# 42 instead of 32 tokens by gathered rows, in three partition groups with three row slots

## The chip, the cores and the metric

The kernel runs on one core of one Trainium2 chip. The metric is the device time of one execution in microseconds (us). Three executions of the kernel before took 2955.79, 2960.62 and 2963.03 us; the median is 2960.62 us. A fourth one, taken by the hardware profiler, took 2955.81 us, and every row below comes from it.

## The reference, cut to what matters

Two transformer blocks are computed for 256 tokens of width 2048, in fp32. The change touches the last layer of the second block only, a mixture of 16384 experts. Each token chooses 16 experts in each of 8 heads, 128 in all, and gets from each a scalar activation and a row of 2048 values:

```python
    def block(args):
        xt, it, gt = args
        u = jnp.take(expert_u, it, axis=0)
        act = jax.nn.gelu(jnp.einsum('td,tkd->tk', xt, u)) * gt
        v = jnp.take(expert_v, it, axis=0)
        return jnp.einsum('tk,tkd->td', act, v)
```

`it` holds the 128 expert numbers of a token and `gt` their gate values. A final norm follows.

## The kernel before

**Two ways to the same layer.** Of the 256 tokens, the first `TD` = 224 go through the dense way: all 16384 experts are multiplied with them on TensorE, and a gate matrix that is zero wherever an expert was not chosen takes the unwanted ones out. The last `TS` = 32 tokens go through the sparse way: only their 128 chosen rows of u and of v are fetched, by gathers, and multiplied on VectorE (DVE).

**The dense way** streams u and v once, in 1 MB tiles (43, 43 and 42 of each, the three `RANGES`). The order is u0, v0, u1, v1, u2, v2, and I call each of these a pass. A tile is four pieces of 128 x 512, so the passes have 172, 172 and 168 pieces. Every fp32 weight is split in two parts, ACT makes the high part (`split_hi`, L266) and DVE the low part (`split_lo`, L274), for two pieces at a time. TensorE then does four pairs of matmuls in each piece. In a pair the high part meets both parts of the tokens, 2 x 224 = 448 columns, and the low part meets the high part of the tokens alone, 224 columns. In u passes that is `wide` (L292, L293), in v passes `experts_out` (L1406, L1408). ACT may split two pieces only when TensorE is done with the piece six before them (`NQ` = 8 pieces are held), and the DVE program puts the low part of piece s + 4 (`LA`) at the head of step s.

**Beside the pieces** each step s of a pass has other work at hand-set places. In u passes DVE adds the partial sums (`dve_u_sum`, L1349) and builds the gates of four tokens at a time (`dve_gates`, L1286 to L1297, `NG` = 56 per pass), and TensorE turns them into the gate matrix (`pe_gates`, L1311). In the first 36 pieces of a v pass DVE multiplies activation and gate (`dve_gated`, L1372, 12 pieces ahead of use) and takes the low part of the product (`dve_act`, L1388, 7 ahead). At 1, 44, 87 and 130 pieces it adds up v results (`dve_v_sum`).

**The sparse way.** 32 tokens stand four times over the 128 partitions, each group with 32 of the 128 experts of its tokens (`ROWS` = 32). One gather (`pool_rows`, L1447, issued by POOL) brings half a row, 4 KB, into each of the 128 partitions; 64 gathers bring u and 64 bring v. The gathered tile goes to one of two ring slots. `dve_rows` multiplies it: L1469 for u with a running sum, L1476 (L1473 the first time) for v. So one gather is one row operation, 128 in all. The next gather into a slot is issued when DVE is done with that slot. DVE does the row operation at its place in the list `PLACES` and not before: 16 and 15 places in u1 and u2, ten pieces apart; 36, 36 and 26 in the v passes, 3.5 pieces apart, of which the first stands 46 pieces into the pass. One of the places (`NROW`) is used to add the dot products, and gelu and gates follow on ACT and DVE. At the end TensorE adds the four groups (`pe_rows_sum`, L1551) and DVE adds the result to the last tokens.

**Queues.** All tiles of weights are issued by SP, in order, into three buffers `raw`; SP waits until the low parts of the tile three before are made. POOL's queue holds nothing but gathers in these passes.

Of the kernel before, what the change touches and what calls it, by code (L numbers as in the profile page):

```python
# [15 lines left out]
TS = 32  # L16
# [12 lines left out]
NR, NQ, LA = 3, 8, 4  # L29
# [84 lines left out]
def build(nc, A, out):  # L114
# [207 lines left out]
    norm_load = [("gp", 16), ("g2", 16), ("ffn_const", 32), ("g5", 16)]  # L322
# [806 lines left out]
    def dve_choice(e, s):  # L1129
# [53 lines left out]
        for n, tb in enumerate((1, 0)):  # L1183
# [14 lines left out]
            if d == 0:  # L1198
                e.wait_ge(S("tk"), TKN * 8)
                if n:  # L1200
                    e.wait_ge(S("sel"), 1)
                    e.wait_ge(S("sp_ix"), 2 + 3 * (128 // TS))
# [44 lines left out]
            elif d == 10 and n == 0:  # L1247
                own, ids = slice(TD - 128, 128), xi
                e.wait_ge(S("dec"), ND)
                e.scalar_tensor_tensor(ids[own, :], I_[own, :], 128.0, J_[own, :], ALU.mult, ALU.add).then_inc(  # L1250
                    S("sp_ix"), 1)
                e.wait_ge(S("sp_ix"), 1)
                e.tensor_scalar(ids[own, :], ids[own, :], 2.0, None, ALU.mult).then_inc(S("sp_ix"), 1)
                e.wait_ge(S("sp_ix"), 2)
                for j in range(128 // TS):
# [999 lines left out]
```

## Time and profile before

| | us |
|---|---|
| median of three runs | 2960.62 |
| profiled execution | 2955.81 |
| its span, first to last instruction | 2954.5 |
| of it, TensorE (PE) busy | 2911.7 |
| DVE busy | 2139.5 |
| ACT busy | 1570.7 |
| POOL busy | 419.0 |

Between the span and the time of the execution lie 1.3 us. A busy TensorE is one with a matmul in its pipeline, so this number says that it seldom stands still, not that it runs at its peak; the distance between the starts of two matmuls tells how fast it goes. The granted clock is 0.997 of full speed over the span. The page names a share of 9% of the chain that ended last for DMA, nearly all of it gathers.

### The profile page before, as it was taken

The page shows a single profiled execution, that of the slowest core. Times are in us where ns is not written, and L with a number is a line of the kernel's source. Part 1 is how long each engine was busy: PE and PEld are TensorE (multiplying, and loading weights), DVE is VectorE, ACT ScalarE, POOL GpSimd, SP SyncE. Part 2 cuts the span into 40 slices and gives each one's busy share as a digit, 9 for nine tenths or more (in the row PEclk, how much of TensorE's full clock was granted, in tenths as well). Part 3 has the DMA queues.
Part 4 walks back from the last instruction along what each step waited for, and adds up shares of the span by engine and source line. Part 5 has one row for each costly group of instructions (what it writes and reads, how often), then busy time and mean ns, then how long its engine had stood idle before and what let it go on. Part 6 is the DMA issues. An engine that isn't in the chain of part 4 may idle for free.

```text
span 2954.5 us, 45739 instructions
## 1 busy us (share of the span) xinstructions
PE 2911.7 (99%) x18502; PEld 2631.0 (89%) x18502; DVE 2139.5 (72%) x3352; ACT 1570.7 (53%) x2406; POOL 419.0 (14%) x304
## 2 busy tenths in 40 slices
PE   9999999999999999999998999999999999999998
PEld 7888888888888888899898999999999999999997
DVE  5566566666666455676589889778999777999776
ACT  4467755555555443577444556444556444556534
POOL 0011101111111000143020000232010133110131
PEclk9999999999999999999999999999999999999999
DMA  7544445555556554654564555788666788666784
GB/s 259 177 151 152 156 177 186 185 186 187 185 186 222 190 198 143 221 177 170 208 211 171 190 183 203 270 302 298 230 236 227 247 306 302 234 232 239 272 310 168
DMA packets 99009, 631.53 MB, mean 214 GB/s; under 512 B 11376, under 2 KB 12784, under 8 KB 31216
## 3 DMA queue, kind: packets, MB, share of 16 engines
q1 hardware_dynamic: 80368, 561.49, 54.3%
q0 software_dynamic: 18432, 67.12, 6.3%
q8 instruction: 148, 2.42, 0.3%
q14 instruction: 61, 0.50, 0.0%
HBM read 623.32 MB, written 4.19 MB: 212 GB/s over the span
## 4 chain that ended last, share of the span: by engine, by line
PE 78%; DMA 9%; DVE 8%; ACT 3%; issue 2%; SPq 0%; ACTq 0%; DVEq 0%
PE ps L292 26%; PE ps L293 13%; PE ps L1406 6%; PE ps L314 6%; PE ps L316 6%; PE ps L315 6%; DMA ring<-in_u_rows_dram,idx 5%; DMA ring<-in_v_rows_dram,idx 4%; PE ps L1408 3%; DVE loR L274 3%; PE ps L305 2%; PE ps L304 2%; PE ps L303 2%; ACT hiR L266 1%; PE ps L1311 1%
## 5 line engine op out<-in xcount | busy, mean ns | idle before, releaser
L274 DVE TENSOR_TENSOR loR<-raw,hiR 128x1024 fp32r<-128x1024 f32 x1017 | 1255.0, 1241 | 621.9 <-ACT hiR L266 618.4
L266 ACT CAST hiR<-raw 128x1024 fp32r<-128x1024 f32 x1026 | 1074.4, 1051 | 803.3 <-PE ps L1408 324.3
L292 PE MATMUL ps<-XA,hiR 128*128 128x448 f32 (+1 forms) x3936 | 1343.9, 391 | 10.7 <-DVE loR L274 9.3
L293 PE MATMUL ps<-XA,loR 128*128 128x224 f32 (+1 forms) x3936 | 1069.3, 272 | 0.0
L292 PEld LDWEIGHTS ps<-XA,hiR 128*128 128x128 f32 x3936 | 739.7, 188 | 127.1 <-DVE loR L274 6.6
L293 PEld LDWEIGHTS ps<-XA,loR 128*128 128x128 f32 x3936 | 747.7, 190 | 0.6
L1406 PE MATMUL ps<-hl,hiR 128*128 128x448 f32 x2048 | 651.0, 377 | 6.2 <-DVE loR L274 5.9
L1408 PE MATMUL ps<-hl,loR 128*128 128x224 f32 x2048 | 543.5, 265 | 0.0
L1406 PEld LDWEIGHTS ps<-hl,hiR 128*128 128x128 f32 x2048 | 385.2, 188 | 42.8 <-DVE loR L274 9.2
L1408 PEld LDWEIGHTS ps<-hl,loR 128*128 128x128 f32 x2048 | 392.1, 191 | 0.2 <-issue 0.2
L1447 POOL DMA_INDIRECT ring<-in_u_rows_dram,idx x64 | 103.2, 1612 | 716.8 <-DVE ring L1469 664.8
L1320 ACT ACTIVATE G__147<-ps 128x172 f32<-128x172 f32 (+1 forms) x168 | 52.9, 315 | 227.8 <-PE ps L1311 227.7
L1447 POOL DMA_INDIRECT ring<-in_v_rows_dram,idx x64 | 105.2, 1644 | 407.9 <-DVE vsum L1476 391.8
L314 PE MATMUL ps<-hiR,Y 128*128 128x512 f32 x344 | 133.8, 389 | 0.0
L315 PE MATMUL ps<-loR,Y 128*128 128x512 f32 x344 | 133.8, 389 | 0.0
L316 PE MATMUL ps<-hiR,Y 128*128 128x512 f32 x344 | 133.8, 389 | 0.0
L1469 DVE SCALAR_TENSOR_TENSOR ring<-ring,hrep 128x1024 f32<-128x1024 f32 x64 | 78.2, 1222 | 54.6 <-DMA ring<-in_u_rows_dram,idx 54.5
L1476 DVE SCALAR_TENSOR_TENSOR vsum<-ring,gated,vsum 128x1024 f32<-128x1024 f32 x62 | 79.5, 1282 | 47.5 <-DMA ring<-in_v_rows_dram,idx 47.4
L303 PE MATMUL ps<-XB,hiR 128*128 128x256 f32 x384 | 110.0, 286 | 0.0
L305 PE MATMUL ps<-XB,loR 128*128 128x256 f32 x384 | 108.6, 283 | 0.0
L304 PE MATMUL ps<-XB,hiR 128*128 128x256 f32 x384 | 108.6, 283 | 0.0
L314 PE MATMUL ps<-hiR,XA 128*128 128x512 f32 x256 | 101.0, 394 | 2.3 <-DVE loR L274 1.8
(307 smaller groups left out, 3490.1 us busy)
## 6 DMA issues: line engine op xcount, KB each, us to landing
raw<-in_u_dram SPq DMA_DIRECT2D x128, 1024.0 KB
raw<-in_v_dram SPq DMA_DIRECT2D x128, 1024.0 KB
raw<-in_w_up_dram SPq DMA_DIRECT2D x86, 1024.0 KB
raw<-in_w_down_dram SPq DMA_DIRECT2D x43, 1024.0 KB
raw<-in_w_in_qk_dram SPq DMA_DIRECT2D x32, 1024.0 KB
raw<-in_w_out_dram SPq DMA_DIRECT2D x32, 1024.0 KB
raw<-in_w_in_dram SPq DMA_DIRECT2D x24, 1024.0 KB
raw<-in_w_in_v_dram SPq DMA_DIRECT2D x16, 1024.0 KB
```

The lines of the kernel that those rows point to most:

```text
L266: e.copy(hiR[:, r:r + 2, :], raw[n % NR][:, q:q + 2, :]).then_inc(S("hi"), 1)
L274: e.tensor_tensor(loR[:, r:r + 2, :], raw[n % NR][:, q:q + 2, :], hiR[:, r:r + 2, :].bitcast(F32), ALU.subtract).then_inc(S("lo_pool" if p ...
L292: e.matmul(both, wh, X.hl[:, :, k, 0:nt], start=(k == 0), stop=False, skip_group_check=True)
L293: m = e.matmul(dst[:, 0:nt], wl, X.h[:, k, 0:nt], start=False, stop=(k == KC - 1), skip_group_check=True)
L303: e.matmul(dst, wh, X.h[:, k, :], start=(k == 0), stop=False)
L304: e.matmul(dst, wh, X.l[:, k, :], start=False, stop=False)
L314: e.matmul(dsts[tb], ah_, hi, start=first, stop=False)
L315: e.matmul(dsts[tb], ah_, lo, start=False, stop=False)
L316: m = e.matmul(dsts[tb], al_, hi, start=False, stop=last)
L1406: e.matmul(b[:, 0:2 * TD].rearrange("p (a t) -> p a t", a=2), wh, hl[:, :, i, :], start=(i == 0), stop=False, skip_group_check=True)
L1408: m = e.matmul(b[:, 0:TD], wl, hl[:, 0, i, :], start=False, stop=(i == i1 - i0 - 1), skip_group_check=True)
L1447: e.indirect_dma_start(ring[m % 2][:, :], None, A["u_rows" if m < NROW else "v_rows"], bass.IndirectOffsetOnAxis(ap=idx[:, m % NROW // 2, ...
```

## The change

`TS` becomes 42 and `TD` 214. Every pair of matmuls in the six passes has 428 + 214 columns instead of 448 + 224, and everything that is shaped by `TD` shrinks with it; the gates come in 54 groups per pass, the last with two tokens.

42 tokens fit three times into 128 partitions, so `GROUPS` is 3, a gather has 126 rows, and each group needs 43 of the 128 experts (3 x 43 = 129, the surplus one has gate 0). That makes 86 + 86 = 172 row operations, 44 more. The ring has three slots (`RN`). The places in u1 and u2 stay. Those in the v passes become 52, 51 and 39; they start 12, 3 and 3 pieces into the pass instead of 46, and stand 3.0, 3.2 and 3.4 pieces apart.

42 is no multiple of 32, so partitions 86 to 127 can't be copied to the groups by DVE. DVE writes indices and gates of all 128 tokens to a staging tile (six instructions instead of twelve), and SP copies them to the groups with six small DMAs. They stand in SP's queue behind the 13th tile of u0, with waits for `x_out` and `sp_ix`. The staging tile lies in the third ring slot. Sums at the end use all 128 partitions, with `sel4` zero where nothing is to be added, and two waits order them (`xacc`, `sp_x`). Two pairs of semaphores at the start of the kernel are merged (`gp` and `ident`; `x0sq` and `x1sq`). The rest of the diff is addresses and names.

```diff
-TS = 32
+TS = 42
...
-NR, NQ, LA = 3, 8, 4
+NR, NQ, LA, RN = 3, 8, 4, 3
...
-ROWS = 128 * TS // 128
+GROUPS = 128 // TS
+GP = GROUPS * TS
+ROWS = -(-128 // GROUPS)
 NROW = 2 * ROWS
 PLACES = [P_U[r] + 4 + 10 * k for r in (1, 2) for k in range((16, 15)[r - 1])]
-PLACES += [P_VV[r] + NI + 3 + int(3.5 * k) for r in range(3) for k in range((36, 36, 26)[r])]
+PLACES += [P_VV[r] + (12, 3, 3)[r] + int((3.0, 3.2, 3.4)[r] * k) for r in range(3) for k in range((52, 51, 39)[r])]
...
-    ring = [at(f"ring{i}", 4 * i, [128, 1024]) for i in range(2)]
-    SG = NI * TD / 256
+    
+    SG = -(-NI * TD // 8) / 32
     S_, G_ = at("S_", RB, [128, NI, TD]), at("G_", RB + SG, [128, NI, TD])
-    hl = at("hl", RB, [128, 2, NI, TD], F32R)
+    hl = at("hl", RB, [128, 2, int(SG * 256)], F32R)[:, :, 0:NI * TD].rearrange("p a (i t) -> p a i t", t=TD)
...
-    yT = [at("yT0", 8, [128, 8, TD]), at("yT1", o + 10.25, [128, 8, TD])]
-    idx = at("idx", 15, [128, ROWS, 2], U32)
-    gs = at("gs", 15.25, [128, ROWS])
-    dots = at("dots", 15.375, [128, ROWS, 2])
-    gated = at("gated", 15.625, [128, ROWS])
+    hrep, vsum = at("hrep", o + HV, [128, D]), at("vsum", o + HV, [128, D])
+    yT = [at("yT0", 8, [128, 8, TD]), at("yT1", o + HV + 8, [128, 8, TD])]
+    idx = at("idx", 14.75, [128, ROWS, 2], U32)
+    gs = at("gs", 15.125, [128, ROWS])
+    dots = at("dots", 15.3125, [128, ROWS, 2])
+    gated = at("gated", 15.6875, [128, ROWS])
+    ring = [at(f"ring{i}", (0, 4, o + HV + 14.75)[i], [128, 1024]) for i in range(RN)]
+    ixs = at("ixs", o + HV + 14.75, [128, GROUPS * ROWS, 2], U32)
+    gss = at("gss", o + HV + 16, [128, GROUPS * ROWS])
     o = RB + SG
     qT = [at(f"qT{i}", o - 16 + i, [128, T]) for i in range(16)]
     g5 = at("g5", o, [128, D])
...
-                own, ids = slice(TD - 128, 128), xi
+                ids = xi
                 e.wait_ge(S("dec"), ND)
-                e.scalar_tensor_tensor(ids[own, :], I_[own, :], 128.0, J_[own, :], ALU.mult, ALU.add).then_inc(
-                    S("sp_ix"), 1)
+                e.scalar_tensor_tensor(ids[:, :], I_[:, :], 128.0, J_[:, :], ALU.mult, ALU.add).then_inc(S("sp_ix"), 1)
                 e.wait_ge(S("sp_ix"), 1)
-                e.tensor_scalar(ids[own, :], ids[own, :], 2.0, None, ALU.mult).then_inc(S("sp_ix"), 1)
+                e.tensor_scalar(ids[:, :], ids[:, :], 2.0, None, ALU.mult).then_inc(S("sp_ix"), 1)
                 e.wait_ge(S("sp_ix"), 2)
-                for j in range(128 // TS):
-                    part, cs = slice(TS * j, TS * j + TS), slice(ROWS * j, ROWS * j + ROWS)
-                    e.tensor_copy(idx[part, :, 0], ids[own, cs]).then_inc(S("sp_ix"), 1)
-                    e.tensor_scalar(idx[part, :, 1], ids[own, cs], 1.0, None, ALU.add).then_inc(S("sp_ix"), 1)
-                    e.tensor_copy(gs[part, :], g_[own, cs]).then_inc(S("sp_ix"), 1)
+                e.tensor_copy(ixs[:, 0:128, 0], ids[:, :]).then_inc(S("sp_ix"), 1)
+                e.tensor_copy(ixs[:, 128:129, 0], ids[:, 127:128]).then_inc(S("sp_ix"), 1)
+                e.tensor_scalar(ixs[:, 0:128, 1], ids[:, :], 1.0, None, ALU.add).then_inc(S("sp_ix"), 1)
+                e.tensor_scalar(ixs[:, 128:129, 1], ids[:, 127:128], 1.0, None, ALU.add).then_inc(S("sp_ix"), 1)
+                e.tensor_copy(gss[:, 0:128], g_[:, :]).then_inc(S("sp_ix"), 1)
+                e.memset(gss[:, 128:129], 0.0).then_inc(S("sp_ix"), 1)
             elif d == 14:
                 e.wait_ge(S("sel_g"), 3 * n + 3)
                 e.scalar_tensor_tensor(selb[:, 3, half(tb)], bank[4][:, 256:384], 4096.0, selb[:, 2, half(tb)],
...
-    NG = TD // 4
+    NG = -(-TD // 4)
...
         if s == min(SLOT) - 14:
-            e.wait_ge(S("sp_ix"), 2 + 3 * (128 // TS))
-            e.wait_ge(S("x_out"), 16)
-            todo = [0, 1]
-        elif m is not None and m + 2 < 2 * NROW:
+            e.wait_ge(S("sp_load"), 32 * GROUPS)
+            todo = list(range(RN))
+        elif m is not None and m + RN < 2 * NROW:
             e.wait_ge(S("sp_use"), m + 1)
-            todo = [m + 2]
+            todo = [m + RN]
         for m in todo:
-            e.indirect_dma_start(ring[m % 2][:, :], None, A["u_rows" if m < NROW else "v_rows"],
-                                 bass.IndirectOffsetOnAxis(ap=idx[:, m % NROW // 2, m % 2:m % 2 + 1], axis=0)).then_inc(
-                S(f"row{m % 2}"), 16)
+            e.indirect_dma_start(ring[m % RN][0:GP, :], None, A["u_rows" if m < NROW else "v_rows"],
+                                 bass.IndirectOffsetOnAxis(ap=idx[0:GP, m % NROW // 2, m % 2:m % 2 + 1],
+                                                           axis=0)).then_inc(S(f"row{m % RN}"), 16)
 
...
-            e.wait_ge(S(f"row{m % 2}"), 16 * (m // 2 + 1))
-            rg, cs = ring[m % 2][:, :], slice(1024 * (m % 2), 1024 * (m % 2) + 1024)
+            e.wait_ge(S(f"row{m % RN}"), 16 * (m // RN + 1))
+            rg, cs = ring[m % RN][0:GP, :], slice(1024 * (m % 2), 1024 * (m % 2) + 1024)
...
-            m = e.matmul(bank[v_bank(2, 2) + f][:, :], sel4[:, :], vsum[:, quarter(f)], start=True, stop=True)
+            m = e.matmul(bank[v_bank(2, 2) + f][:, :], sel4[0:GP, :], vsum[0:GP, quarter(f)], start=True, stop=True)
...
+            if f >= 2 and tb:
+                e.wait_ge(S("sp_x"), 4)
...
-        load(e, "ident", ident[:, :], A["ident"])
+        load(e, "gp", ident[:, :], A["ident"])
...
-                for j in range(128 // TS):
+                for j in range(GROUPS):
                     load(e, "hrep", hrep[TS * j:TS * j + TS, :], tmp3[TD - 128:128, 1, :])
+            elif n == P_U[0] // 4 + 12:
+                e.wait_ge(S("x_out"), 16)
+                e.wait_ge(S("sp_ix"), SP_IX)
+                for j in range(GROUPS):
+                    own, to, cs = slice(TD - 128, 128), slice(TS * j, TS * j + TS), slice(ROWS * j, ROWS * j + ROWS)
+                    load(e, "sp_load", idx[to, :, :], ixs[own, cs, :])
+                    load(e, "sp_load", gs[to, :], gss[own, cs])
             elif n == P_VV[2] // 4 + 4:
```

What the change does to the queues, at three places. TensorE first, at the end of u0 and the start of v0; before:

```order
L293 MATMUL ps<-XA,loR 128x224
L292 MATMUL ps<-XA,hiR 128x448
L293 MATMUL ps<-XA,loR 128x224
L1406 MATMUL ps<-hl,hiR 128x448
L1408 MATMUL ps<-hl,loR 128x224
```

and now:

```order
L300 MATMUL ps<-XA,loR 128x214
L299 MATMUL ps<-XA,hiR 128x428
L300 MATMUL ps<-XA,loR 128x214
L1415 MATMUL ps<-hl,hiR 128x428
L1417 MATMUL ps<-hl,loR 128x214
```

The order is the same, and each matmul is narrower. (`XA` and `hl` are the tokens' side, `hiR` and `loR` the weights.)

DVE at the start of v1, from one low part to the next. `G_` is the product of activation (`S_`) and gate, `hl` its two parts. Before:

```order
L274 TENSOR_TENSOR loR<-raw_50,hiR 128x1024
L1349 TENSOR_TENSOR S__146<-S__146,ps 128x224
L1372 TENSOR_TENSOR G__147<-S__146,G__147 128x224
L1388 TENSOR_TENSOR hl<-G__147,hl 128x224
L1372 TENSOR_TENSOR G__147<-S__146,G__147 128x224
L1388 TENSOR_TENSOR hl<-G__147,hl 128x224
L274 TENSOR_TENSOR loR<-raw_51,hiR 128x1024
```

and now:

```order
L281 TENSOR_TENSOR loR<-raw_50,hiR 128x1024
L1358 TENSOR_TENSOR S__144<-S__144,ps 128x214
L1381 TENSOR_TENSOR G__145<-S__144,G__145 128x214
L1397 TENSOR_TENSOR hl<-G__145,hl 128x214
L1381 TENSOR_TENSOR G__145<-S__144,G__145 128x214
L1397 TENSOR_TENSOR hl<-G__145,hl 128x214
L1477 SCALAR_TENSOR_TENSOR ring_166,dots<-ring_166,hrep 126x1024
L281 TENSOR_TENSOR loR<-raw_51,hiR 128x1024
```

A row operation has come in between two low parts, in the stretch in which each piece also has its two operations on `G_` and `hl`.

POOL, from the last work of the layer before to the first gathers, with the semaphores that each waits for; before:

```order
L274 TENSOR_TENSOR loR<-raw_51,hiR 128x1024 [waits s_hi]
L1447 DMA ring_144<-in_u_rows_dram,idx 128x1024 [waits s_x_out,s_sp_ix]
L1447 DMA ring_145<-in_u_rows_dram,idx 128x1024
L1447 DMA ring_144<-in_u_rows_dram,idx 128x1024 [waits s_sp_use]
L1447 DMA ring_145<-in_u_rows_dram,idx 128x1024 [waits s_sp_use]
```

and now:

```order
L281 TENSOR_TENSOR loR<-raw_51,hiR 128x1024 [waits s_hi]
L1455 DMA ring_164<-in_u_rows_dram,idx 126x1024 [waits s_sp_load]
L1455 DMA ring_165<-in_u_rows_dram,idx 126x1024
L1455 DMA ring_166<-in_u_rows_dram,idx 126x1024
L1455 DMA ring_164<-in_u_rows_dram,idx 126x1024 [waits s_sp_use]
L1455 DMA ring_165<-in_u_rows_dram,idx 126x1024 [waits s_sp_use]
```

Three gathers go out before the first wait for DVE, and the first of them waits for SP's small DMAs.

## Rows read from the trace of the kernel before

**Rows 1.** The page: busy time of TensorE; the high-part group of ACT.

```profile
PE 2911.7 (99%) x18502; PEld 2631.0 (89%) x18502; DVE 2139.5 (72%) x3352; ACT 1570.7 (53%) x2406; POOL 419.0 (14%) x304
...
L266 ACT CAST hiR<-raw 128x1024 fp32r<-128x1024 f32 x1026 | 1074.4, 1051 | 803.3 <-PE ps L1408 324.3
```

**Rows 2.** Six passes: us, PE, PEld, DVE, ACT, POOL busy, PEclk, DMA share, GB/s.

```profile
1565.00:1816.00 251.00, 241.76 (x1836) 223.33 (x1837) 220.82 (x472) 134.73 (x252) 2.05 (x2) 0.99 0.54 185
1816.00:2037.00 221.00, 218.46 (x1379) 206.20 (x1378) 167.86 (x230) 100.24 (x121) 59.24 (x35) 1.00 0.79 285
2037.00:2271.00 234.00, 232.31 (x1824) 216.25 (x1823) 218.07 (x353) 128.71 (x236) 24.85 (x17) 1.00 0.68 234
2271.00:2495.00 224.00, 220.73 (x1382) 208.01 (x1381) 170.67 (x211) 99.95 (x122) 60.41 (x35) 0.99 0.78 282
2495.00:2722.00 227.00, 227.00 (x1793) 211.63 (x1793) 211.93 (x329) 125.97 (x232) 22.62 (x15) 1.00 0.68 232
2722.00:2941.00 219.00, 218.64 (x1377) 205.21 (x1376) 164.43 (x191) 100.54 (x131) 47.22 (x27) 1.00 0.72 259
```

**Rows 3.** Timeline of TensorE, wide pairs of an earlier layer: start, us, instruction; five starts.

```profile
699.61 0.40 PE L292 MATMUL ps<-XA,hiR 128*128 128x512 f32 x1
...
701.02 0.40 PE L292 MATMUL ps<-XA,hiR 128*128 128x512 f32 x1
```

**Rows 4.** The same view in v2; thirteen starts of L1406, first and last.

```profile
2740.09 0.38 PE L1406 MATMUL ps<-hl,hiR 128*128 128x448 f32 x1
...
2743.87 0.38 PE L1406 MATMUL ps<-hl,hiR 128*128 128x448 f32 x1
```

**Rows 5.** The same view in u1, around the matmuls of one gate group.

```profile
2180.38 0.37 PE L1311 MATMUL ps<-OG,OJ 128*128 128x43 f16 x8
2180.59 0.45 PE L292 MATMUL ps<-XA,hiR 128*128 128x448 f32 x1
```

**Rows 6.** Waits of TensorE over the six passes: us, times, longest.

```profile
PE ps L292 <- DVE loR L274: 9.0, 10, 1.8
PE ps L1406 <- DVE loR L274: 5.9, 7, 2.7
```

**Rows 7.** Timeline of DVE at the start of v0, two pieces.

```profile
1820.84 1.22 DVE L274 TENSOR_TENSOR loR<-raw,hiR 128x1024 fp32r<-128x1024 f32 x1
1821.97 0.39 DVE L1372 TENSOR_TENSOR G__147<-S__146,G__147 128x224 f32<-128x224 f32 x1
1822.28 0.39 DVE L1388 TENSOR_TENSOR hl<-G__147,hl 128x224 fp32r<-128x224 f32 x1
...
1823.18 1.22 DVE L274 TENSOR_TENSOR loR<-raw,hiR 128x1024 fp32r<-128x1024 f32 x1
```

**Rows 8.** Timeline of DVE in u2, around one row operation.

```profile
2502.30 1.28 DVE L1476 SCALAR_TENSOR_TENSOR vsum<-ring,gated,vsum 128x1024 f32<-128x1024 f32 x1
2503.50 1.22 DVE L274 TENSOR_TENSOR loR<-raw,hiR 128x1024 fp32r<-128x1024 f32 x1
```

**Rows 9.** The chain through v0: gathers from release to landing, shortest and longest of twelve.

```profile
1907.85 6.50 DMA ring<-in_u_rows_dram,idx
...
1944.09 10.08 DMA ring<-in_u_rows_dram,idx
```

**Rows 10.** Waits over v0 (1816 to 2036 us): waits of DVE for gathers.

```profile
DVE ring L1469 <- DMA ring<-in_u_rows_dram,idx: 38.4, 20, 5.8
```

**Rows 11.** DMA view, 1900 to 2030 us of v0: GB/s in 40 slices; packets, MB, share of engines.

```profile
GB/s 290 272 302 387 325 263 349 326 224 386 232 287 277 393 261 401 277 52 408 425 306 403 335 117 382 295 325 378 146 239 418 343 334 425 218 417 328 342 418 90
...
q1 hardware_dynamic: 3488, 25.34, 52.4%
q0 software_dynamic: 4086, 14.84, 31.7%
```

**Rows 12.** DMA view, first 40 us of the kernel: GB/s in slices of 1 us.

```profile
GB/s 0 57 172 426 459 401 410 426 467 366 461 426 401 418 483 393 410 333 228 262 418 355 392 377 412 389 410 434 442 98 8 0 0 0 16 172 418 410 401 393
```

More of the change, by code:

```diff
@@ L227, in build @@
     fl = [at(f"fl{i}", o + 34.375 + i / 2, [128, 128]) for i in range(8)]
+    assert BASE + (RB + 2 * SG + 4.25 + HV + 18.75) * KB <= 224 * KB
     S_BUSY = int((SG - 16) * 256 / TD)
@@ L321, in build @@
     norm_gain = [gp, g2, g4, g5]
-    norm_load = [("gp", 16), ("g2", 16), ("ffn_const", 32), ("g5", 16)]
+    norm_load = [("gp", 32), ("g2", 16), ("ffn_const", 32), ("g5", 16)]
     norm_to = [XA, XA, XB, XA]
@@ L377, in pe_norm_first @@
         if i == 0:
-            e.wait_ge(S("ident"), 16)
+            e.wait_ge(S("gp"), 32)
         for q in range(TURN_FIRST[i]):
@@ L1074, in build @@
     TKN = 36
+    SP_IX = 8
     DEC0 = TK0 + 8 * TKP + 2
@@ L1319, in act_gates @@
             e.wait_ge(S("g_mm"), k + 1)
-            e.mul(G_[:, 0:ni, 4 * n:4 * n + 4], bank[b][:, 0:4 * ni].rearrange("p (t i) -> p i t", t=4),
+            w = min(4, TD - 4 * n)
+            e.mul(G_[:, 0:ni, 4 * n:4 * n + w], bank[b][:, 0:w * ni].rearrange("p (t i) -> p i t", t=w),
                   1.0 / 4096).then_inc(S("g_ev"), 1)
@@ L1337, in act_u_part @@
         if r == 0 and i == 0:
-            e.wait_ge(S("hrep"), 16 * (128 // TS))
+            e.wait_ge(S("hrep"), 16 * GROUPS)
         elif r == 0 and i == S_BUSY:
@@ L1467, in dve_rows @@
                 if m == 0:
-                    e.wait_ge(S("hrep"), 16 * (128 // TS))
-                e.scalar_tensor_tensor(rg, rg, 1.0, hrep[:, cs], ALU.mult, ALU.mult,
-                                       accum_out=dots[:, j, m % 2:m % 2 + 1]).then_inc(S("sp_use"), 1)
+                    e.wait_ge(S("hrep"), 16 * GROUPS)
+                e.scalar_tensor_tensor(rg, rg, 1.0, hrep[0:GP, cs], ALU.mult, ALU.mult,
+                                       accum_out=dots[0:GP, j, m % 2:m % 2 + 1]).then_inc(S("sp_use"), 1)
             elif j == 0:
-                e.wait_ge(S("sp_a"), 1)
-                e.tensor_scalar(vsum[:, cs], rg, gated[:, 0:1], None, ALU.mult).then_inc(S("sp_use"), 1)
+                e.wait_ge(S("sp_g"), 3)
+                e.tensor_scalar(vsum[0:GP, cs], rg, gated[0:GP, 0:1], None, ALU.mult).then_inc(S("sp_use"), 1)
             else:
                 e.wait_ge(S("sp_use"), m - 1)
-                e.scalar_tensor_tensor(vsum[:, cs], rg, gated[:, j:j + 1], vsum[:, cs], ALU.mult, ALU.add).then_inc(
+                e.scalar_tensor_tensor(vsum[0:GP, cs], rg, gated[0:GP, j:j + 1], vsum[0:GP, cs], ALU.mult, ALU.add).then_inc(
                     S("sp_use"), 1)
@@ L1555, in dve_rows_sum @@
         e.wait_ge(S("sp_sum"), 1)
-        own = slice(TD - 128, 128)
         e.wait_ge(S("end_const"), 48)
+        e.wait_ge(S("xacc"), 4)
         for f in range(4):
-            e.tensor_tensor(xr[own, 1, quarter(f)], xr[own, 1, quarter(f)], bank[v_bank(2, 2) + f][own, :],
+            e.tensor_tensor(xr[:, 1, quarter(f)], xr[:, 1, quarter(f)], bank[v_bank(2, 2) + f][:, :],
                             ALU.add).then_inc(S("sp_x"), 1)
@@ L1730, in act_program @@
         e.wait_ge(S("x0"), 16)
-        e.activation(tmp0[:, 0, :], x[:, 0, :], ACT.Square, accum_out=ss[:, 0:1]).then_inc(S("x0sq"), 1)
-        e.wait_ge(S("x0sq"), 1)
-        e.wait_ge(S("x1sq"), 1)
+        e.activation(tmp0[:, 0, :], x[:, 0, :], ACT.Square, accum_out=ss[:, 0:1]).then_inc(S("xsq"), 1)
+        e.wait_ge(S("xsq"), 2)
         act_root(e, 0, ss)
@@ L1879, in dve_program @@
         e.scalar_tensor_tensor(tmp0[:, 1, :], x[:, 1, :], 1.0, x[:, 1, :], ALU.mult, ALU.mult,
-                               accum_out=ss[:, 1:2]).then_inc(S("x1sq"), 1)
+                               accum_out=ss[:, 1:2]).then_inc(S("xsq"), 1)
         dve_root(e, 0, ss)
@@ L2156, in _constants @@
     c["mul_dl"] = m
-    c["sel4"] = (TD - 128 + k % TS == q).astype(f)
+    c["sel4"] = ((TD - 128 + k % TS == q) & (k < GP)).astype(f)
     c["am_dl"] = np.where(m > 0, 0.0, NEG)
```

18 lines of the change are left out of this document (9 added, 9 removed).

## The prediction

> **What bounds the kernel now.** I read the page first for who is busy, then the six passes one by one, then the distances between starts of matmuls, and last the waits of TensorE and the gathers. TensorE has a matmul in its pipeline for 2911.7 of 2954.5 us [rows 1]; so the question is how fast it goes and where it stands. In the plain part of v2 thirteen starts of the high-part matmul lie 3.78 us apart, twelve pairs, 0.315 us each [rows 4]. A piece is four pairs, 1.26 us; 172 pieces make 216.7 us and 168 make 211.7. The v passes take 221, 224 and 219 us [rows 2], so they lose about 4, 7 and 7 us. Of the last 7 I put some 5 down to the summing and turning matmuls at the end, which stay. A gate group costs u1 and u2 about 0.29 us: 0.21 to the next start, and the matmul behind it holds 0.08 longer than usual [rows 5]. 56 of them and 172 pieces give 233 us, and u1 took 234. So the passes run at the pace of TensorE with small losses, and only u0, at 251 us, is some 18 us over, because DVE also does the choice of experts there. TensorE waited for the low part 9.0 us in u and 5.9 us in v passes [rows 6]. DVE is busy 218 of 234 us in u1 and 212 of 227 in u2, but only 168, 171 and 164 in the v passes [rows 2]: there is room in v passes, and hardly any in u passes.
>
> **Columns.** A pair of 768 columns takes 1.41 / 4 = 0.3525 us [rows 3], one of 672 takes 0.315 [rows 4]: 0.39 ns a column. The change takes 30 columns from each pair, 11.7 ns. 512 pieces in the u passes and 512 in the v passes, four pairs each, are 4096 pairs and give **47.9 us**. Bounds: if all of a pair's time were columns, 0.315 x 30 / 672 = 14.1 ns and 57.6 us; if the narrow matmul could not get shorter, two thirds of 11.7 ns and 31.9 us. I take the slope, since the trace has both widths. Six gate groups fewer give 6 x 0.29 = 1.7 us more.
>
> **What u passes do not give back.** In the stretch of u0 where DVE sets the pace, narrower matmuls bring nothing. Its 18 us of loss lie over some 27 pieces, by what is left of the pass, so 27 x 0.047 = 1.3 us are not gained; with the carry I take off 2.0. In u1 and u2 DVE was at 93% [rows 2]. Its low parts and gates keep their length while the pass shrinks by 8.6 us, so it stands at 96 to 97%. That still fits, but a late piece is made up more slowly; I take off 1.5 us (0 to 5).
>
> **Row operations, where DVE has no room.** At the start of a v pass DVE needs 2.34 us for two pieces: 1.13 for the low part and four times 0.30 [rows 7]. TensorE took 2.52. Now it is 1.13 + 4 x 0.29 = 2.30 against 2.42, 0.12 us of slack. This is where new row operations stand, 1.20 us each by the distance to the next instruction [rows 8]; the kernel before had none ahead of piece 46. Up to piece 30 there are 7 in v0, 9 (the tenth at 31) in v1 and 9 in v2. DVE falls behind by 7 x 1.2 - 1.1 = 7.3 us, 10 x 1.2 - 1.7 = 10.3 and 9 x 1.2 - 1.6 = 9.2. From there to piece 36 it about holds, and behind 36 it catches up. TensorE doesn't feel the first part of that. ACT starts the high part six pieces ahead, 6 x 1.21 = 7.3 us; 1.05 [rows 1] and 1.13 go for the two parts, so DVE can be late by 5.1 us, and I take 4.6 since it isn't always fully ahead. What is left is 2.7 + 5.7 + 4.6 = **13.0 us lost**. Bounds: 0 if SP, ACT and DVE have more lead than that, 26.8 if they have none. The low part is at the head of a step and the row operation at its end, so a full allowance is the nearer one. Behind these places nothing else is short: in the middle of a pass, three pieces hold 1.5 low parts and one row operation, 2.9 of 3.64 us.
>
> **Waits for gathers.** Before, DVE had 2 x 3.5 x 1.26 - 1.2 = 7.6 us from giving back a slot to needing it, and a gather needed 6.5 to 10.1 us [rows 9]; over 36 row operations in v0 DVE waited 38.4 us [rows 10], 1.1 each. Most of it was covered by the same allowance, and 4 + 7 + 2 = 13 us of TensorE's losses in v passes are what can be won. With three slots it is 3 x 3.0 x 1.21 - 1.2 = 9.7 us in v0, 10.4 in v1 and 11.1 in v2. If gathers took as long as now, waits would nearly be gone. But the DMA engines get more to do. By [rows 11], 25.34 MB are 24.2 tiles and cost 0.524 x 16 x 130 us of engines, 45.1 engine-us each; 14.84 MB are 28.3 gathers, 23.3 each. Three pieces and a gather in v0 then want 33.8 + 22.9 = 56.7 of 16 x 3.64 = 58.2 engine-us, 97%; v1 95%, v2 93%; before it was 62.8 of 70.6, 89%. In bytes v0 wants 217 + 142 = 359 GB/s. The slices go to 425 [rows 11], and the first 30 us of the kernel hold about 410 [rows 12], so 359 is to be had, with longer gathers. I take half: **6 us won**, of 0 to 13.
>
> **Moved and added small things.** Six small DMAs stand in SP's queue behind a tile fetch; the fetch of the next tile stands behind them. Their wait for the indices ends at step 22 of u0, and the 13th tile is asked for at about step 34, so it is over by then, and the gathers that wait for them are needed some 150 pieces later. DVE writes six staging instructions instead of twelve. At the start, the norm now waits for `ident` too, which TensorE waited for anyway. All nothing, up to 1 us.
>
> **The sum.** 47.9 + 1.7 - 2.0 - 1.5 - 13.0 + 6 = 39.1 us. From 2955.8, the profiled execution, this gives 2916.7. The median of the runs shown is 4.8 us above that execution; in the same proportion the forecast is **2921 us**, with a range of its own of 2910 to 2934.
>
> **Rivals.** *Everything covered:* the lag of DVE meets more lead and the waits go. That is worth 8 us of the 13.0 and 7 of the 13 more: 2906. For it speaks that DVE was seldom what TensorE waited for; against it that 1.2 us are put where 0.12 are free.
>
> *The narrow matmul doesn't shrink:* its weight load or a fixed part sets its length. 16 us less gained: 2937. Against it speaks that 96 columns fewer brought 0.0375 us.
>
> *A gather of 126 rows uses fewer engines.* 128 rows are 8 for each of 16 engines; 126 are 9 for each of 14. On these 14, v0 would want 22.9 x 16 / 14 + 33.8 = 60.0 of 58.2 engine-us and v1 100%. Over 190 us of v0 that adds 6 us and in v1 1: 2928. The rows give no engine numbers, so the trace speaks neither way. The Trainium skill ("DMA: Bandwidth & Descriptors", section "Why a DMA increments its semaphore by 16 and not by 1") says that a transfer is split over the largest number of engines up to 16 that divides its partitions, and that gathers by POOL take such engines in turn. By that rule the split is 14, but the load evens out over the 16, and only each gather gets longer, by one packet in nine; the trace can't agree or disagree.
>
> *The DMA engines give no more than they gave,* 40.2 MB in 130 us, 309 GB/s [rows 11]. v0 has 45.1 + 26.8 = 71.9 MB to bring, v1 70.9: 233 and 229 us, 17 more than before; v2 gives 5 and the u passes 22. That is -10: 2950.
>
> *Slower:* three gathers in flight take engines from the tiles, tiles come late, and the total falls. All v passes have 207 MB, and they would have to take 664 + 22 = 686 us to eat the gain of the u passes, 302 GB/s. At 295 they take 702: 2976. Against it speak the slices above 400 and the start of the kernel; for it, only that the sum of shares comes to 97%.
>
> **Chances.** Forecast 0.64, everything covered 0.10, fewer engines 0.08, narrow matmul 0.06, DMA as before 0.08, slower 0.04. Since v0 is so near the limit, the range goes up to 2946 and leaves out the last two; down it goes to 2902, past the covered case. A measurement of this kernel can tell 0.3%, 9 us, from no change. Faster by more has 0.92, as the DMA case may end on either side of that line, same 0.04, slower 0.04.
>
> **What would show it.** In the profile of the changed kernel, starts of high-part matmuls 0.303 us apart in the plain part of v passes, u1 and u2 at about 226 and 219 us. Between pieces 15 and 36 of v1 and v2, TensorE waits for the low part with DVE without idle time, 5.7 and 4.6 us; later in the pass there is little. DVE's waits for gathers fall from 38 us in v0 to below 20 while GB/s there goes to about 350. It is wrong if TensorE waits in the middle of v0 with DVE idle on a gather or ACT on a tile: then the DMA engines are the bound. It is wrong the other way if DVE's lag at piece 36 is never seen by TensorE.

## The result: slower, 3025 us instead of the 2921 forecast

The changed kernel took 3024.98 us in the median of five runs (3019.49 to 3031.89), beside 2955.79 for the kernel before in the same session. The ratio is 1.0228, with an interval of 1.0206 to 1.0250. The forecast was 2921 us with a range up to 2946, so it missed the sign too. The profiled execution has a span of 3018.1 us against 2954.5.

The pass table of the changed kernel, in the same columns as [rows 2] (us, then PE, PEld, DVE, ACT and POOL busy, PEclk, DMA share, GB/s), for u0, v0, u1, v1, u2, v2:

```profile
1565.00:1811.00 246.00, 236.43 (x1824) 223.74 (x1824) 217.09 (x460) 132.87 (x250) 3.39 (x3) 0.99 0.56 191
1811.00:2065.00 254.00, 223.94 (x1375) 214.06 (x1374) 185.11 (x264) 97.73 (x121) 86.64 (x52) 0.96 0.95 278
2065.00:2293.00 228.00, 227.41 (x1813) 217.09 (x1812) 212.79 (x344) 127.74 (x236) 24.09 (x16) 1.00 0.71 242
2293.00:2544.00 251.00, 227.41 (x1375) 216.20 (x1374) 184.16 (x230) 97.26 (x122) 81.76 (x50) 0.95 0.95 279
2544.00:2767.00 223.00, 221.88 (x1776) 211.69 (x1775) 208.46 (x324) 125.29 (x231) 22.89 (x15) 1.00 0.71 238
2767.00:3005.00 238.00, 220.04 (x1381) 207.43 (x1379) 178.59 (x205) 99.07 (x132) 87.18 (x39) 0.99 0.88 264
```

The u passes fell from 251, 234 and 227 to 246, 228 and 223 us, 15 us in all. The v passes rose from 221, 224 and 219 to 254, 251 and 238, 79 us. The last two columns point at the cause. The DMA engines are busy for 95% of v0 and v1, and yet bring 278 GB/s, less than the 285 they brought there before with a share of 0.79. They are full, and they are slow.

The waits over v0 (waiter <- releaser: us in total, times, longest), where [rows 10] had 38.4 us for the gathers:

```profile
ACT hiR L273 <- DMA raw<-in_v_dram: 105.4, 29, 5.1
DVE ring L1477 <- DMA ring<-in_u_rows_dram,idx: 67.5, 25, 5.3
PE ps L1415 <- DVE loR L281: 29.9, 13, 4.4
```

ACT now waits for tiles of weights and DVE for gathers, one behind the other, and TensorE for the low parts that come late. The DMA view of the middle of v0, over the same stretch as [rows 11] (GB/s in 40 slices, then packets, MB and share of the engines by queue, last the median us from issue to landing):

```profile
GB/s 308 340 272 294 233 329 297 272 287 251 257 299 281 248 262 248 271 250 324 258 313 232 299 320 323 246 305 248 300 290 266 314 271 271 305 343 247 316 213 349
...
q1 hardware_dynamic: 3055, 22.15, 56.5%
q0 software_dynamic: 4547, 14.65, 42.1%
...
raw<-in_v_dram SPq DMA_DIRECT2D x22, 1024.0 KB, 10.5
ring<-in_u_rows_dram,idx POOLq DMA_INDIRECT x29, 12.0
```

22.15 MB are 21.1 tiles, and 0.565 x 16 x 130 us by 21.1 is 55.7 engine-us for a tile (45.1 before). 14.65 MB are 28.4 gathers, 30.8 engine-us each (23.3 before). The slices, which reached 425 GB/s before, stay at 349 or less. A gather takes 12.0 us from issue to landing, a tile 10.5.

What was left to find: is it the shape of the gathers (126 rows instead of 128), their density and the third slot, or DVE at the start of the v passes? Theory A is the shape, B the load, C is DVE. (An engine-us is one of the 16 DMA engines busy for 1 us.)

### The profile page after: what moved, and what is told of

Same layout as the page of the kernel before. It is cut to its first block, busy times and chain, and to the rows that moved or that the text cites. A ratio compares the mean times of both kernels' runs of the same rounds, so it can differ in the third digit from the quotient of the medians.

```text
span 3018.1 us, 45745 instructions
## 1 busy us (share of the span) xinstructions
PE 2909.7 (96%) x18454; PEld 2650.8 (88%) x18454; DVE 2170.7 (72%) x3394; ACT 1558.5 (52%) x2400; POOL 508.0 (17%) x348
## 4 chain that ended last, share of the span: by engine, by line
PE 66%; DMA 15%; DVE 13%; ACT 3%; issue 2%; SPq 0%; ACTq 0%; DVEq 0%
PE ps L299 24%; PE ps L300 12%; DMA ring<-in_v_rows_dram,idx 8%; PE ps L321 6%; PE ps L323 6%; PE ps L322 6%; DMA ring<-in_u_rows_dram,idx 6%; DVE loR L281 5%; PE ps L311 3%; PE ps L310 3%; PE ps L312 3%; DVE ring L1477 2%; ACT hiR L273 1%; PE ps L1319 1%; DVE vsum L1484 1%
## 5 line engine op out<-in xcount | busy, mean ns | idle before, releaser
L299 PE MATMUL ps<-XA,hiR 128*128 128x428 f32 (+1 forms) x3936 | 1328.0, 388 | 11.7 <-DVE loR L281 9.6
L300 PE MATMUL ps<-XA,loR 128*128 128x214 f32 (+1 forms) x3936 | 1068.0, 271 | 0.0
L1415 PE MATMUL ps<-hl,hiR 128*128 128x428 f32 x2048 | 661.4, 383 | 71.6 <-DVE loR L281 71.4
L1417 PE MATMUL ps<-hl,loR 128*128 128x214 f32 x2048 | 544.7, 266 | 0.0
L1415 PEld LDWEIGHTS ps<-hl,hiR 128*128 128x128 f32 x2048 | 397.1, 194 | 103.4 <-DVE loR L281 65.2
L1455 POOL DMA_INDIRECT ring<-in_u_rows_dram,idx x86 | 137.5, 1599 | 669.2 <-DVE ring L1477 593.4
L1455 POOL DMA_INDIRECT ring<-in_v_rows_dram,idx x86 | 160.4, 1865 | 427.0 <-DVE vsum L1484 402.7
L1484 DVE SCALAR_TENSOR_TENSOR vsum<-ring,gated,vsum 126x1024 f32<-126x1024 f32 x84 | 107.6, 1281 | 88.7 <-DMA ring<-in_v_rows_dram,idx 88.5
L1477 DVE SCALAR_TENSOR_TENSOR ring<-ring,hrep 126x1024 f32<-126x1024 f32 x86 | 104.9, 1220 | 77.2 <-DMA ring<-in_u_rows_dram,idx 76.9
L844 POOL TENSOR_TENSOR acc<-acc,acc 128x256 f32<-128x256 f32 x43 | 31.7, 738 | 475.6 <-DVE acc L798 475.6
```

Source lines behind the costliest of these rows:

```text
L299: e.matmul(both, wh, X.hl[:, :, k, 0:nt], start=(k == 0), stop=False, skip_group_check=True)
L300: m = e.matmul(dst[:, 0:nt], wl, X.h[:, k, 0:nt], start=False, stop=(k == KC - 1), skip_group_check=True)
L1415: e.matmul(b[:, 0:2 * TD].rearrange("p (a t) -> p a t", a=2), wh, hl[:, :, i, :], start=(i == 0), stop=False, skip_group_check=True)
L1417: m = e.matmul(b[:, 0:TD], wl, hl[:, 0, i, :], start=False, stop=(i == i1 - i0 - 1), skip_group_check=True)
L1455: e.indirect_dma_start(ring[m % RN][0:GP, :], None, A["u_rows" if m < NROW else "v_rows"], bass.IndirectOffsetOnAxis(ap=idx[0:GP, m % NROW ...
```

## Experiment 1: gathers of 128 rows in the changed kernel

```diff
-            e.indirect_dma_start(ring[m % RN][0:GP, :], None, A["u_rows" if m < NROW else "v_rows"],
-                                 bass.IndirectOffsetOnAxis(ap=idx[0:GP, m % NROW // 2, m % 2:m % 2 + 1],
+            e.indirect_dma_start(ring[m % RN][:, :], None, A["u_rows" if m < NROW else "v_rows"],
+                                 bass.IndirectOffsetOnAxis(ap=idx[:, m % NROW // 2, m % 2:m % 2 + 1],
...
+                load(e, "sp_load", idx[GP:128, :, :], ixs[GP:128, 0:ROWS, :])
```

The two partitions more get valid indices, and what they bring is used nowhere; the wait for `sp_load` grows by 16.

> The changed kernel with one thing undone: each gather brings 128 rows again, 8 for each of 16 DMA engines, instead of 126. Indices for partitions 126 and 127 come with one more small DMA; what they bring isn't used. Theory A (the shape of the gather: 126 rows make each packet of a gather and of the tiles slower, 30.8 and 55.7 engine-us per gather and tile in v0 instead of 23.3 and 45.1): nearly all of the loss goes, 2915 to 2935 us. Theory B (load: 52, 51 and 39 gathers with three in flight saturate the DMA engines whatever their shape): no change or a few us slower by the 1.6% more bytes, 3015 to 3035 us. Theory C (DVE is late at the start of v passes): no change, 3015 to 3030 us.

Measured: 2924.39 us (2918.82 to 2926.14), ratio 0.9891 with an interval of 0.9849 to 0.9934 against the kernel before. Two rows more in each gather, 1.6% more bytes, and the whole loss is gone. A second set of runs of this kernel, taken on one chip with another experiment below, gave 2922.36 us and 0.9895 (0.9873 to 0.9916):

> The first experiment's kernel (gathers of 128 rows, places of the change) on the same chip as the one before, for the comparison: 2920 to 2928 us.

Its v passes, in the columns of the table above (v0 begins 2.4 us after the start of its window, so it takes 215 us):

```profile
1808.00:2025.00 217.00, 215.29 (x1389) 208.09 (x1388) 187.50 (x271) 100.94 (x124) 86.09 (x52) 1.00 0.88 333
2252.00:2469.00 217.00, 213.38 (x1375) 205.92 (x1374) 185.77 (x231) 99.62 (x122) 81.82 (x50) 1.00 0.90 330
2691.00:2909.00 218.00, 214.94 (x1380) 205.93 (x1379) 180.12 (x205) 100.58 (x132) 91.81 (x39) 1.00 0.79 289
```

and 1900 to 2030 us of it by queue:

```profile
q1 hardware_dynamic: 3883, 28.28, 57.5%
q0 software_dynamic: 4941, 17.94, 34.9%
```

A tile costs 44.3 engine-us here and a gather 21.2, no more than before the change (45.1 and 23.3), and 46 MB go through in 130 us, 357 GB/s. So the DMA engines can do what this kernel asks for. The shape decides, for the gather and for the tiles beside it. Theory B falls as the cause of the loss, and so does C.

## Experiment 2: gathers of 126 rows in the kernel before

The mirror of the first. The row operations work on 126 partitions too, so that the share of two partitions is left out.

```diff
-            e.indirect_dma_start(ring[m % 2][:, :], None, A["u_rows" if m < NROW else "v_rows"],
-                                 bass.IndirectOffsetOnAxis(ap=idx[:, m % NROW // 2, m % 2:m % 2 + 1], axis=0)).then_inc(
+            e.indirect_dma_start(ring[m % 2][0:126, :], None, A["u_rows" if m < NROW else "v_rows"],
+                                 bass.IndirectOffsetOnAxis(ap=idx[0:126, m % NROW // 2, m % 2:m % 2 + 1], axis=0)).then_inc(
```

> The kernel before with gathers of 126 rows instead of 128, and the row operations on 126 partitions; the two last partitions' share of the sparse tokens is left out. Two slots, 3.5 pieces apart, nothing ahead of piece 46: neither density nor a third slot. Theory A (shape): in the row stretches a gather costs about 30 engine-us instead of 23.3 and a tile more than 45, which is over 100% there: 2970 to 3000 us. Theory B2 (the shape matters only together with the denser gathers): 2950 to 2965 us.

Measured: 2993.05 us (2985.75 to 3001.44), ratio 1.0129 (1.0096 to 1.0161). By queue, 1900 to 2030 us, and two waits over the six passes:

```profile
q1 hardware_dynamic: 3155, 23.02, 52.8%
q0 software_dynamic: 4081, 13.18, 34.7%
```

```profile
DVE ring L1469 <- DMA ring<-in_u_rows_dram,idx: 75.5, 34, 6.9
PE ps L1406 <- DVE loR L274: 30.7, 20, 4.4
```

13.18 MB are 25.5 gathers of 28.3 engine-us, a tile costs 50.0. TensorE waits 30.7 us instead of 5.9 [rows 6]. The shape alone, without more gathers and without a third slot, costs 38 us. Theory A holds in both kernels.

## Experiment 3: the changed kernel without gathers

```diff
-        elif m is not None and m + RN < 2 * NROW:
-            e.wait_ge(S("sp_use"), m + 1)
-            todo = [m + RN]
...
-            e.wait_ge(S(f"row{m % RN}"), 16 * (m // RN + 1))
+            if m < RN:
+                e.wait_ge(S(f"row{m % RN}"), 16)
+            else:
+                e.wait_ge(S("sp_use"), m - RN + 1)
...
```

The first three gathers stay. The u operation adds instead of multiplying, in the same shape, since the slots are never filled anew.

> The changed kernel with only the first three gathers; all 172 row operations stay at their places and work on what the slots hold, so the sparse tokens' result is left out. The u operation adds instead of multiplying, with the same shapes. It measures columns and DVE without the DMA load. Theory A and B: the loss is all DMA, so this gives the column gain less what DVE costs at the start of v passes: about 2900 to 2912 us, with TensorE waiting for the low part some 13 us in all. Theory C (DVE is the cause): still 2990 us or more.

Measured: 2921.83 us (2920.46 to 2922.41), ratio 0.9886 (0.9845 to 0.9927). Theory C falls here too. The time lies 10 us above the range expected for A and B, since the columns gained less than forecast. With full gathers the kernel is only 2.6 us slower than without any, which is within the spread of the runs, so at 128 rows nearly all of the DMA work is hidden. The run also prices two other terms. The first is the pair of matmuls, over long unbroken stretches, before (191 starts) and here (228 starts of L1415):

```profile
2734.72 0.38 PE L1406 MATMUL ps<-hl,hiR 128*128 128x448 f32 x1
...
2794.72 0.38 PE L1406 MATMUL ps<-hl,hiR 128*128 128x448 f32 x1
```

```profile
2379.77 0.37 PE L1415 MATMUL ps<-hl,hiR 128*128 128x428 f32 x1
...
2449.73 0.37 PE L1415 MATMUL ps<-hl,hiR 128*128 128x428 f32 x1
```

60.00 / 190 = 0.3158 us and 69.96 / 227 = 0.3082 us: a pair got shorter by 7.6 ns, not by 11.7. Over 4096 pairs that is 31 us. The mean distances between starts over the v passes of both traces tell which matmul it was: from the wide one to the narrow one 213.8 ns before and 210.1 now, from the narrow one to the next wide one 102.4 and 98.8. The second term is that TensorE waited for low parts in the v passes:

```profile
PE ps L1415 <- DVE loR L281: 7.7, 15, 0.8
```

With no gather in the way, this is DVE's own lag. 1.2, 3.6 and 2.9 us of it lie in v0, v1 and v2, and of these 0.7, 2.5 and 2.7 in the first 44 us, some 36 pieces, where 2.7, 5.7 and 4.6 were forecast: the right places and about half the size.

## Experiment 4: two slots, with 126 and with 128 rows

```diff
-NR, NQ, LA, RN = 3, 8, 4, 3
+NR, NQ, LA, RN = 3, 8, 4, 2
```

In the changed kernel:

> The changed kernel with two ring slots instead of three; places and gathers of 126 rows stay. Theory A: a gather still takes 12 us and only two are under way, so a row operation comes every 6.7 us at best instead of 4.5, 142 of them in the v passes: clearly slower than the changed kernel, 3080 us or more. Theory B (the third gather in flight is what floods the DMA engines): gathers take 8 to 9 us again and the time stays or falls, 2990 to 3030 us. Theory C: near 3025 us or a little more.

Measured: 3047.39 us (3038.45 to 3052.52), ratio 1.0302 (1.0257 to 1.0348). Without the third gather in flight it is slower by some 22 us, so the third slot isn't the cause of the loss. But no theory's number was hit. The loss is smaller than A's, since a gather takes less time when fewer are under way: in the chain through v0 5.67 to 11.60 us from release to landing, 8.4 in the mean, where the changed kernel has 12.7 to 16.6. This much of theory B is right. With gathers of 128 rows:

> The changed kernel with gathers of 128 rows and two ring slots instead of three. It tells what the third slot is worth once the gathers are quick. If a gather takes 8.7 us from release to landing as in the kernel before, a row operation comes every (8.7 + 1.5) / 2 = 5.1 us where the places ask for 3.64, so v0 takes some 52 x 1.5 = 70 us longer less what the allowance covers: 3000 us or more. If gathers get quicker when fewer are in flight (6.5 us, the shortest before), it is 4.0 us for 3.64: 2935 to 2950 us.

Measured: 2985.82 us (2978.97 to 2997.9), ratio 1.0108 (1.0078 to 1.0139). Neither number was hit, and the first was nearer. In its chain the gathers need between these two, from release to landing:

```profile
1914.87 5.00 DMA ring<-in_u_rows_dram,idx
...
1959.71 9.74 DMA ring<-in_u_rows_dram,idx
```

Eighteen of them stand in the chain from 1880 to 2060 us. So the third slot is worth some 62 us when the gathers are quick and 22 when they are slow. It is needed: places 3.0 pieces apart can't be fed from two slots.

## Experiment 5: other numbers of rows

In the changed kernel `GP`, the number of partitions for gathers and row operations, is set by hand; the rest of the sparse tokens' share is left out.

```diff
-GP = GROUPS * TS
+GP = 112
```

and 120, 124, 64 and 96. The question is whether the number of DMA engines explains it.

> The changed kernel with gathers and row operations on 112 partitions, 16 engines with 7 rows each; the last 14 partitions' share is left out. Theory A1 (a gather is split over the largest number of engines up to 16 that divides its rows, and is slow when that isn't 16): 112 is clean, packets as quick as with 128 rows, 2918 to 2930 us. Theory A2 (any gather that isn't 128 rows is slow): about 3000 to 3020 us, a little less than with 126 rows for the fewer bytes.

> The same with 120 partitions, 15 engines with 8 rows each by theory A1. A1 gives something between 2930 and 3020 us, with the count of the 4-byte packets per gather unlike the 16 of 128 rows. A2 gives 3005 to 3025 us.

> The same with 124 partitions. By theory A1 only 4 divides it (31 rows on each of 4 engines), so a gather takes 31 packets of 0.16 us or more one after another, 5 us alone and far more between tiles: above 3080 us. By A2 it is like 126 rows: 3015 to 3035 us.

> The changed kernel with gathers and row operations on 64 partitions, 4 for each of 16 engines; the rest of the sparse tokens' share is left out. 64 = 16 x 4 and 4 is the half of the 8 rows of a full gather. If what makes packets slow is that an engine's rows do not start at a multiple of 4 partitions (112 rows are 7 for each engine, 126 are 9, 120 are 8 on 15 engines), a gather of 64 is quick: 11 to 12 engine-us, half of the 21.6 of 128 rows. If any gather short of 128 rows is slow, it is 15 engine-us or more. Time 2915 to 2925 us either way for the smaller load.

> The same with 96 partitions, 6 for each of 16 engines, so no engine but every second starts at a multiple of 4. By the alignment theory slow: 22 engine-us or more for a gather (three quarters of 21.6 would be 16.2), and 2935 to 2965 us. If the number of bytes alone counts, 16.2 and 2918 to 2925 us.

The gather queue's line of the page for 112, 120, 124, 64 and 96 rows in this order (packets, MB, share of 16 engines' span):

```profile
q0 software_dynamic: 22016, 78.92, 9.4%
```

```profile
q0 software_dynamic: 24768, 84.56, 10.9%
```

```profile
q0 software_dynamic: 88064, 87.63, 12.2%
```

```profile
q0 software_dynamic: 13760, 45.10, 5.9%
```

```profile
q0 software_dynamic: 19264, 67.64, 8.2%
```

The same line of the changed kernel, of the kernel before and of experiment 2:

```profile
q0 software_dynamic: 27520, 88.79, 10.6%
```

```profile
q0 software_dynamic: 18432, 67.12, 6.3%
```

```profile
q0 software_dynamic: 20480, 66.08, 7.3%
```

The table follows from them, with the spans of these executions and 172 gathers (128 in the kernel before and in experiment 2). A gather's cost is share x 16 x span, divided by the number of gathers. The last column but one is the mean time of the gathers' 4 KB packets alone, read from the same traces.

| rows | packets per gather | engine-us per gather | per row | 4 KB packet, ns | time, us |
|---|---|---|---|---|---|
| 128, before | 144 = 16 x (8 + 1) | 23.3 | 0.182 | 181 | 2956 |
| 128, changed (experiment 1) | 144 | 22.8 | 0.178 | 177 | 2924 |
| 126, changed | 160 = 16 x (9 + 1) | 29.8 | 0.236 | 234 | 3025 |
| 126, before (experiment 2) | 160 | 27.3 | 0.217 | 213 | 2993 |
| 124 | 512 = 16 x (31 + 1) | 38.7 | 0.312 | 281 | 3409 |
| 120 | 144 = 16 x (8 + 1) | 30.8 | 0.256 | 254 | 3036 |
| 112 | 128 = 16 x (7 + 1) | 26.0 | 0.232 | 229 | 2972 |
| 96 | 112 = 16 x (6 + 1) | 22.5 | 0.235 | 233 | 2945 |
| 64 | 80 = 16 x (4 + 1) | 16.1 | 0.251 | 246 | 2929 |

The times of 124 and 96 rows are as expected by A1 and by the alignment theory; those of 112, 120 and 64 lie outside every range. Two effects come apart.

**How many engines.** The packets per gather are 16 times (rows per engine + 1), if the rows go to the largest number of engines up to 16 that divides them: 31 on 4 engines for 124, 9 on 14 for 126, 8 on 15 for 120, 7, 6 and 4 on 16. The counts fit all seven sizes. The engines left out seem to get packets of 4 bytes instead: the traces have 16 of these per gather with 128, 112, 96 and 64 rows, and 24, 34 and 388 with 120, 126 and 124, which is one more for every row that a left-out engine would have brought. The traces don't name the engines, but of a gather of 124 rows that is alone in its queue never more than 6 packets of 4 KB are under way at once, where other sizes mostly have 16 or more. With 124 rows a gather is slowest to land, since each engine brings 31 rows one after the other: 31 x 0.281 = 8.7 us, and the lone ones move their rows in 8.9 us at the median, those of 126 rows in 2.6:

```profile
DVE ring L1477 <- DMA ring<-in_u_rows_dram,idx: 211.6, 29, 17.8
```

That is DVE waiting in v0 and most of u1 (1811 to 2400 us), up to 17.8 us at a time; the one execution took 3409 us. The Trainium skill ("DMA: Bandwidth & Descriptors", section "Why a DMA increments its semaphore by 16 and not by 1") says that the split takes the largest divisor up to 16. With that rule the traces agree: 512 packets at 124 rows and 160 at 126 come out of it, where rows spread as evenly as possible over 16 engines would give 144 for both.

**How slow a packet is.** It isn't the number of engines. 112, 96 and 64 rows use 16 engines evenly, and yet a row costs 0.23 to 0.25 engine-us where 128 rows cost 0.18. 112 rows bring 12.5% fewer bytes than 128 and make the kernel 47 us slower. The theory with which I chose 64 and 96, that an engine's rows must start at a multiple of 4 partitions, falls too: 64 rows are 4 for each engine, 11 to 12 engine-us were expected and 16.1 came. (64 rows also fill only one half of the partitions, so this run doesn't clear every account by partitions.) What is left is that only gathers over all 128 partitions were quick. The tiles beside them suffer as well: 55.7 engine-us instead of 45 beside gathers of 126 rows.

The packets' own times narrow it down. The quickest 4 KB packets take 156 to 159 ns in every kernel. With 128 rows 88 to 91% of them take at most 165 ns, with 126 rows and three slots 25%, with 64 to 124 rows 13 to 37%. The number in flight counts too: with two slots it is 45 to 53% for 126 rows. So a packet of the other shapes isn't slow in itself; many are held up, by something that gathers over 128 partitions meet far less. The Trainium skill (the same page, section "The descriptor swizzle") says that with 128 partitions each engine's eight rows lie on one port of the memory. If a split with another number of rows doesn't keep to that, engines would meet at ports; no run here shows ports, so this stays a guess. What holds the packets up is open.

## Experiment 6: the places moved

On top of experiment 1:

```diff
-PLACES += [P_VV[r] + (12, 3, 3)[r] + int((3.0, 3.2, 3.4)[r] * k) for r in range(3) for k in range((52, 51, 39)[r])]
+PLACES += [P_VV[r] + (12, 14, 14)[r] + int((3.0, 3.05, 3.2)[r] * k) for r in range(3) for k in range((52, 51, 39)[r])]
```

> The changed kernel with gathers of 128 rows, as in the first experiment, and one more edit: the places of the v passes start 12, 14 and 14 pieces in (were 12, 3, 3), 3.0, 3.05 and 3.2 apart. If the rest of the loss in v1 and v2 is DVE's lag from row operations among the activations (TensorE waited 2.5 + 1.2 us there in v1 and 2.9 + 1.1 in v2), three row operations fewer in each of these stretches win 4 to 8 us against the same kernel with the places of the change: 2915 to 2920 us. If it is the DMA load, the closer places cost a few us: 2924 to 2932 us.

Measured: 2916.50 us (2911.58 to 2923.38), ratio 0.9875 (0.9855 to 0.9894). The same kernel with the places of the change had 2922.36 on the same chip, ratio 0.9895 (0.9873 to 0.9916). The intervals overlap, so 6 us are likely and not shown. From 2252 to 2330 us, the start of v1, TensorE waited for low parts

```profile
PE ps L1415 <- DVE loR L281: 0.7, 1, 0.7
```

where it had waited, with the places of the change,

```profile
PE ps L1415 <- DVE loR L281: 3.6, 8, 0.8
```

so the lag went where it was meant to go in v1. In v2 (2688 to 2780 us) it did not: 3.6 us against 3.0. This is the fastest kernel of the study, 1.25% faster than the one before.

## Why the prediction was wrong

**The step that failed** is the price of a gather in "Waits for gathers". It took a gather of 126 rows as 126/128 of one of 128, 22.9 engine-us, and a tile as 45.1. They were 30.8 and 55.7 in v0. With these, three pieces and a gather want 41.8 + 30.8 = 72.6 of 58.2 engine-us, 125%, where the text had 97%. (With the costs of experiment 1 the same sum is 33.2 + 21.2 = 54.4, 93%: it was right for whole gathers.) The engines gave only 278 GB/s, and v0 with its 71.9 MB takes 259 us at that rate; it took 254. The rest follows: in the chain through v0 gathers take 12.7 to 16.6 us from release to landing instead of 6.5 to 10.1, DVE waits, low parts and tiles come late, and TensorE stands. It is the first sign of being wrong that the prediction named. Experiments 1 and 2 show the cause from both sides; why the packets are held up stays open.

**The rival "fewer engines"** had the right property, the number of rows, and its split fits the packet counts, but it stood at a chance of 0.08 and 6 to 7 us. And the number of engines isn't what costs the time: 112, 96 and 64 rows go over all 16 and are slow. It counted only that nine packets go where eight went. That a packet lasts longer, and that tiles pay too, was in no row of the trace, because all gathers there had 128 rows. That was the place to bound from both sides, and the text assumed unchanged packets without a reason. **The rival "slower"** had the right mechanism at its end (the total falls below 302 GB/s, tiles come late) with a wrong cause, three gathers in flight: in experiment 1 three in flight do no harm, and in experiment 4 the third slot is worth more than it costs. Its chance of 0.04 was far too small beside a sum that stood at 97%.

**Columns.** 47.9 us forecast, 31 by the long stretches. The slope from 768 to 672 columns did not carry on to 642. The size is that of the lower bound (31.9), but not for its reason. The rival said that the narrow matmul doesn't shrink; it lost 3.6 ns for its 10 columns, about what the slope gives (3.9), and the wide one lost only 3.7 ns for 20 (7.8 by the slope). Why is open.

**u passes.** They gained 15 us in all (5, 6 and 4), and 19 in experiment 1, from the first wide matmul of each pass to the last (250.9, 234.0 and 226.9 us before, then 245.1, 226.2 and 221.3). The forecast had about 22. The columns gave 8 us less there, and the 3.5 us taken off for DVE don't show.

**DVE at the start of v passes.** 13.0 us forecast; 7.7 over whole v passes without gathers. The mechanism and the places are right, the size was not. Either the lead that covers the lag is larger than the 4.6 us taken or DVE falls less behind; no run tells which.

**The third slot.** Forecast as 6 us won, from before's losses. With whole gathers the DMA side costs 2.6 us against no gathers at all. What it cost in the kernel before no run tells, so how much of the possible 13 us was won isn't shown. DVE's waits for gathers in v0 fell from 38.4 to 30.6 and 26.6 us in the two profiles of experiment 1, not to below 20.

**The sum.** Experiment 1 gave 2924 and 2922 us where 2921 was forecast, and that match is luck. The sum promised 39.1 us, and the two sets gained 30.5 and 29.1 us on the kernel before, measured beside them. The forecast started from 2960.62 us, the median of three runs; five runs gave 2955.79. Columns and gate groups alone make 31 + 1.7 = 33 us, and the profiled spans of experiment 1 are 31.2 and 32.4 us shorter than before, that of experiment 3 33.4. So the other terms (-2.0, -1.5, -13.0 and +6) came to about nothing together, and not to -10.5.

**A cost nobody named.** TensorE's granted clock is 0.96 in v0 and 0.95 in v1 of the changed kernel, where both kernels otherwise have 0.99 or 1.00: it stood still often, and the clock went to the lower level (1.2 GHz) for 20 us of v0 and 27 us of v1, in short stretches. Experiment 1 has 1.00 in all v passes. So a stall here costs more than its own length: from its first pair to its last v0 takes 40.5 us longer than in experiment 3, and TensorE's waits for low parts make 29.9 of them; 20 us at half the clock are an estimated 10 more.

## What to carry to other kernels

Gather over all 128 partitions, even if some rows are thrown away: two rows more took 3.3% off this kernel's time. When a change alters the shape of a DMA, its packets' time is not to be scaled by bytes; treat it as unknown, and try the full shape beside it. And when the engines' time comes to 97% of a stretch, the case in which they don't keep up is a main case and not a rival.

## What the runs showed of the hardware that was not expected

- A gather of 4 KB rows costs 0.18 engine-us per row with 128 rows and 0.22 to 0.26 with 126, 120, 112, 96 or 64, and it slows other transfers down: a 1 MB tile goes from 45 to 56 engine-us beside gathers of 126 rows.
- The quickest 4 KB packet takes 156 to 159 ns whatever the shape, but only gathers of 128 rows have some nine in ten of their packets (88 to 91%) near that pace.
- The 512 packets of a gather of 124 rows fit a split over 4 engines, and the kernel takes 3409 us instead of 2922 with 128.
- DMA engines that are busy for 0.95 of the time brought 278 GB/s in one kernel, and with a share of 0.93 357 GB/s in another; the share alone doesn't tell how near the bound is.
- A pair of fp32 matmuls lost 7.6 ns by 30 columns fewer at 672, where 96 fewer at 768 had brought 0.39 ns a column; the wide matmul of the pair is the one that fell short of the slope.
